# A decoder layer on one core: the FFN's down projection as seven block products, with operand sums made on GpSimd

## What is computed

```python
    x = x + mixed @ w_out[l]
    h2 = rmsnorm(x, norm_ffn_g[l])
    gate = causal_dwconv(h2 @ w_gate[l], ffn_conv_w[l]) + ffn_conv_b[l]
    x = x + (jax.nn.silu(gate) * (h2 @ w_up[l])) @ w_down[l]
return rmsnorm(x, norm_final_g)
```

## Time and profile before

| | us |
|---|---|
| median of three runs | 1390.34 (1389.62 to 1392.69) |
| the profiled execution | 1392.53 |
| its span, first to last instruction | 1390.7 |
| PE busy | 1318.5 (95%) |
| DVE busy | 863.5 (62%) |
| ACT busy | 576.2 (41%) |
| POOL busy | 332.6 (24%) |

### The profile page before, as it was taken

The page is one execution under the profiler, slowest core; times in us unless marked ns, Lnnn a source line. Parts: engine busy times, 40 slices in busy tenths (PEclk is TensorE's granted clock), DMA queues, the critical chain, the costliest instruction groups (busy, mean ns, idle before and its releaser), DMA issues.

```text
span 1390.7 us, 17095 instructions
## 1 busy us (share of the span) xinstructions
PE 1318.5 (95%) x6366; PEld 1076.2 (77%) x6366; DVE 863.5 (62%) x1195; ACT 576.2 (41%) x1028; POOL 332.6 (24%) x248
## 2 busy tenths in 40 slices
PE   7999999988888899889997999999999999999996
PEld 6788888876667687768886788888888878888885
DVE  6433352179887888654458888877777873345442
ACT  6211121078777787532353333333333332234330
POOL 0100100033131321100065455545445410001010
PEclk9999999999999999999999999999999999999998
DMA  5111112000000000143112222122222248435631
GB/s 220 53 45 45 61 46 91 0 20 1 1 1 1 1 2 1 49 169 131 63 40 80 91 74 75 64 91 91 74 78 92 76 157 298 157 118 167 202 97 61
DMA packets 37965, 110.75 MB, mean 80 GB/s; under 512 B 4016, under 2 KB 4528, under 8 KB 37680
## 3 DMA queue, kind: packets, MB, share of 16 engines
...
...
## 4 chain that ended last, share of the span: by engine, by line
PE 74%; DVE 13%; issue 6%; ACT 5%; POOL 1%; DMA 1%; DVEq 0%; SPq 0%; ACTq 0%; POOLq 0%
PE PS L496 9%; PE PS L497 8%; PE PS L500 8%; PE PS L2037 6%; PE PS L2039 6%; PE PS L2038 6%; PE PS L2049 6%; PE PS L2051 6%; PE PS L2050 6%; PE PS L1902 3%; DVE wl L1560 3%; ACT F L1053 2%; PE PS L1919 2%; DVE nmax L1439 2%; PE PS L1854 2%
## 5 line engine op out<-in xcount | busy, mean ns | idle before, releaser
L496 PE MATMUL PS<-R,wh 128*128 128x512 f32 x560 | 222.7, 398 | 13.7 <-DVE wl L488 13.7
L497 PE MATMUL PS<-R,wh 128*128 128x512 f32 x560 | 219.7, 392 | 0.0
L2037 PE MATMUL PS<-R,wh 128*128 128x512 f32 x480 | 189.3, 394 | 13.6 <-DVE wl L1560 8.4
L2038 PE MATMUL PS<-R,wh 128*128 128x512 f32 x480 | 188.1, 392 | 0.0
L2039 PE MATMUL PS<-R,wl 128*128 128x512 f32 x480 | 187.9, 392 | 0.0
L500 PE MATMUL PS<-R,wl 128*128 128x512 f32 x560 | 173.8, 392 | 0.0
L2049 PE MATMUL PS<-R,wh 128*128 128x512 f32 x352 | 137.5, 390 | 0.0
L2051 PE MATMUL PS<-R,wl 128*128 128x512 f32 x352 | 137.0, 389 | 0.0
L2050 PE MATMUL PS<-R,wh 128*128 128x512 f32 x352 | 137.0, 389 | 0.0
L496 PEld LDWEIGHTS PS<-R,wh 128*128 128x128 f32 x560 | 106.3, 190 | 37.6 <-DVE wl L488 14.6
L497 PEld LDWEIGHTS PS<-R,wh 128*128 128x128 f32 x560 | 106.3, 190 | 22.5 <-issue 0.7
...
## 6 DMA issues: line engine op xcount, KB each, us to landing
...
```

The lines of the kernel that those rows point to most:

```text
L496: nc.tensor.matmul(out, w_h, hi(kt)[:, cols], start=first, stop=False)
L497: nc.tensor.matmul(out, w_h, lo(kt)[:, cols], start=False, stop=False)
L2037: nc.tensor.matmul(out, w_h, operand(name, k, 0), start=fresh and k == 0, stop=False, skip_group_check=not fresh)
L2038: nc.tensor.matmul(out, w_h, operand(name, k, 1), start=False, stop=False, skip_group_check=not fresh)
```

## The change

The down projection is also done as 2 x 2 blocks in seven block products. The blocks are halves: the 22 tiles f pair up to eleven (even and odd tile of a pair are the two block rows of the inner dimension), the outputs split into d = 0 to 3 and 4 to 7, and the tokens into LEFT and RIGHT. Each of the seven products runs over the eleven pairs, so there are 77 steps, each of a 128 x 512 weight piece and a 128 x 512 activation piece, with four output banks and twelve matmuls. Products 0, 2, 4 and 6 add up in banks 0 to 3 without a clear, and 1, 3 and 5 use banks 4 to 7. DVE adds a bank group into the residual's quarters in the first steps of the next product, 28 additions of 128 x 512 before the last four; before it was 16 in all.

The weight sums S1 to S4 are made by POOL for the eleven pairs, at the very start and in the convolution stage behind L782: load two weight units (1 MB) by a DMA of its own queue into `R2`, four 128 x 512 operations, store the sums (1 MB) to DRAM. ACT waits for all the stores before it first writes `R2`. The activation sums T1 to T4 of a gated pair are made by POOL behind the S sums of m odd (`act_sums`): four 128 x 512 operations out of `SA`, then two DMA stores of 512 KB. ACT's silu of the next pair waits for them. SP stores three quarters of each pair (256 KB each) in place of two tiles, and SP's fetch of the residual now also waits for the last activation sums.

The splits run three steps ahead in place of two, in a ring of six half slots for the weights.

```diff
+        DOWN = (("A11", "B11"), ("S1", "T1"), ("S2", "T2"), ("S4", "B22"), ("S3", "T3"), ("A12", "B21"), ("A22", "T4"))
+        STEPS_DOWN = NP * PAIRS
+        TAIL_K = 4
+        HALF_D = KT // 2
+        D1, D3 = F1[:, 4, LEFT], F1[:, 4, RIGHT]
+        D2, D4 = PBm[:, 1024:1024 + BANK], PBm[:, 1024 + BANK:2048]
...
+        act_dram = nc.dram_tensor("gated", (NP, PAIRS, P, BANK), F32).ap()
+        s_dram = nc.dram_tensor("weight_sums", (PAIRS, P, 4 * BANK), F32).ap()
...
+            if v < SLOTS:
+                eng.wait_ge(p_done, NP * MATRICES + v - SLOTS + 1)
             else:
-                eng.wait_ge(dw_done, u - 4 + 1)
+                eng.wait_ge(dw_done, v - SLOTS + 1)
...
+            if v == 0:
+                return [2, 3]
+            if v == STEPS_DOWN - 5:
+                return [v + 3, v + 4]
+            return [n for n in [v + 3] if n < STEPS_DOWN - 1]
...
+                done = a_last if p == PAIRS - 1 else a_out
                 sp.wait_ge(a_ready, count)
-                sp.dma_start(a_dram[2 * p + e], SA[e]).then_inc(a_last if p == PAIRS - 1 else a_out, 16)
+                if e:
+                    sp.dma_start(act_dram[3][p], SA[1][:, LEFT]).then_inc(done, 16)
+                    sp.dma_start(act_dram[5][p], SA[1][:, RIGHT]).then_inc(done, 16)
+                else:
+                    sp.dma_start(act_dram[0][p], SA[0][:, RIGHT]).then_inc(done, 16)
...
             def load_down(v):
-                if v < 2:
+                q, k = divmod(v, PAIRS)
+                name = DOWN[q][0]
+                if v < 4:
                     sp.wait_ge(p_lo, NP * (MATRICES - 1))
-                elif v < 4:
-                    sp.wait_ge(p_lo, NP * MATRICES)
                 else:
                     sp.wait_ge(dw_lo, v - 3)
-                n = DOWN0 + v % FT if v < 2 * FT else LAST0 + v - 2 * FT
-                sp.dma_start(down_raw(v)[:, down_columns(v)], w_units[n][:, down_columns(v)]).then_inc(down_in[v % 4], 16)
+                if name[0] == "S":
+                    src = s_dram[k][:, (int(name[1]) - 1) * BANK:int(name[1]) * BANK]
+                else:
+                    src = w_units[DOWN0 + 2 * k + (name[2] == "2")][:, RIGHT if name[1] == "2" else LEFT]
+                sp.dma_start(down_raw(v), src).then_inc(down_in[v % 4], 16)
 
             def load_a(n):
+                q, k = divmod(n, PAIRS)
                 if n < 4:
                     sp.wait_ge(p_lo, NP * MATRICES)
                 else:
                     sp.wait_ge(da_lo, n - 3)
                 if n == 0:
-                    sp.wait_ge(a_out, 32 * (PAIRS - 1))
-                if n == FT - 2:
-                    sp.wait_ge(a_last, 32)
-                sp.dma_start(a_raw(n), a_dram[n % FT][:, half_of(n // FT)]).then_inc(a_in[n % 4], 16)
-
-            for v in range(3):
+                    sp.wait_ge(a_out, 48 * (PAIRS - 1))
+                if n == PAIRS - 1:
+                    sp.wait_ge(a_last, 48)
+                if n == PAIRS:
+                    sp.wait_ge(dt_out, 32 * (PAIRS - 1))
+                if n == 2 * PAIRS - 1:
+                    sp.wait_ge(dt_last, 32)
+                sp.dma_start(a_raw(n), act_dram[q][k]).then_inc(a_in[n % 4], 16)
...
+            for v in range(4):
                 load_down(v)
+            for v in range(4):
                 load_a(v)
...
                 if 6 <= v < 6 + KT:
                     if v == 6:
                         sp.wait_ge(p_done, NP * MATRICES)
-                        sp.wait_ge(a_last, 32)
+                        sp.wait_ge(a_last, 48)
+                        sp.wait_ge(dt_made, 4 * PAIRS)
                     sp.dma_start(x2(v - 6), x1_dram[v - 6]).then_inc(x1_back, 16)
...
+            def load_weights(p):
+                at = 4 * (p % 2)
+                pool.dma_start(W2[:, at:at + 2, :], w_units[DOWN0 + 2 * p:DOWN0 + 2 * p + 2].rearrange("u p n -> p u n"))\
+                    .then_inc(ws_in[p % 2], 16)
+
+            def weight_sums(p):
+
+                at = 4 * (p % 2)
+                a11, a21, a12, a22 = (W2[:, at + n, cols] for n in (0, 1) for cols in (LEFT, RIGHT))
+                s1, s2, s3, s4 = (W2[:, at + n, cols] for n in (2, 3) for cols in (LEFT, RIGHT))
+                pool.wait_ge(ws_in[p % 2], 16 * (p // 2 + 1))
+                if p > 1:
+                    pool.wait_ge(ws_out[p % 2], 16 * (p // 2))
+                nc.gpsimd.tensor_tensor(s1, a21, a22, ALU.add).then_inc(ws_made, 1)
+                nc.gpsimd.tensor_tensor(s3, a11, a21, ALU.subtract).then_inc(ws_made, 1)
+                pool.wait_ge(ws_made, 4 * p + 1)
+                nc.gpsimd.tensor_tensor(s2, s1, a11, ALU.subtract).then_inc(ws_made, 1)
+                pool.wait_ge(ws_made, 4 * p + 3)
+                nc.gpsimd.tensor_tensor(s4, a12, s2, ALU.subtract).then_inc(ws_made, 1)
+                pool.wait_ge(ws_made, 4 * p + 4)
+                pool.dma_start(s_dram[p], W2[:, at + 2:at + 4, :].rearrange("p u n -> p (u n)")).then_inc(ws_out[p % 2], 16)
+                if p + 2 < PAIRS:
+                    load_weights(p + 2)
+
+            load_weights(0)
+            load_weights(1)
+            weight_sums(0)
             pool.wait_ge(r_ready, 2)
             for i in range(CONV_T):
                 pool.wait_ge(conv_ready, i + 1)
                 nc.gpsimd.tensor_tensor(F1[:, CT_S, :], F1[:, CT_S, :], F1[:, R_S, :], ALU.mult).then_inc(tapr_ready, 1)
+                for p in range(1 + 3 * i - (i > 0), min(PAIRS, 3 + 3 * i)):
+                    weight_sums(p)
...
+            def act_sums(p):
+
+                pool.wait_ge(a_ready, folded(p, 4) if p else 2)
+                if p:
+                    pool.wait_ge(dt_out, 32 * p)
+                nc.gpsimd.tensor_tensor(D1, SA[0][:, LEFT], SA[0][:, RIGHT], ALU.subtract).then_inc(dt_made, 1)
+                nc.gpsimd.tensor_tensor(D3, SA[1][:, LEFT], SA[0][:, LEFT], ALU.subtract).then_inc(dt_made, 1)
+                pool.wait_ge(dt_made, 4 * p + 1)
+                nc.gpsimd.tensor_tensor(D2, SA[1][:, LEFT], D1, ALU.subtract).then_inc(dt_made, 1)
+                pool.wait_ge(dt_made, 4 * p + 3)
+                nc.gpsimd.tensor_tensor(D4, SA[1][:, RIGHT], D2, ALU.subtract).then_inc(dt_made, 1)
+                pool.wait_ge(dt_made, 4 * p + 4)
+                done = dt_last if p == PAIRS - 1 else dt_out
+                pool.dma_start(act_dram[1:5:3, p].rearrange("a p n -> p a n"),
+                               F1[:, 4, :].rearrange("p (a n) -> p a n", a=2)).then_inc(done, 16)
+                pool.dma_start(act_dram[2:7:4, p].rearrange("a p n -> p a n"),
+                               PBm[:, 1024:2048].rearrange("p (a n) -> p a n", a=2)).then_inc(done, 16)
...
             for m in range(0, MATRICES, 2):
                 for j in range(1, 5):
                     sum_of(m + 1, j)
+                act_sums(m // 2)
                 if m + 2 < MATRICES:
                     for j in range(1, 5):
                         sum_of(m + 2, j)
                 spread_silu(m + 3, 1)
                 spread_silu(m + 4, 0)
+            act_sums(PAIRS - 1)
+            pool.wait_ge(dt_last, 32)
...
+            act.wait_ge(ws_out[0], 16 * ((PAIRS + 1) // 2))
+            act.wait_ge(ws_out[1], 16 * (PAIRS // 2))
             for k in range(CONV_T):
                 act.wait_ge(yn_ready, k + 1)
                 nc.scalar.activation(R2[:, k, :], F1[:, Y0 + k, :], ACT.Copy).then_inc(mc_hi, 1)
...
                 if p:
-                    act.wait_ge(a_out, 32 * p)
+                    act.wait_ge(a_out, 48 * p)
+                    act.wait_ge(dt_made, 4 * p)
                 nc.scalar.activation(SA[e], T1[e], ACT.Silu).then_inc(silu_ready, 1)
...
+                if q and k == 0:
+                    dve.wait_ge(dw_done, q * PAIRS)
+                if q == 1 and k < 4:
+                    add_down(k, k, RIGHT)
+                if q == 2 and k < 8:
+                    add_down(4 + k % 4, k, LEFT)
+                if q == 3 and k < 4:
+                    add_down(k, k, LEFT, before=ADDS_OF_P1 + k + 1)
+                if q == 4 and k < 4:
+                    add_down(4 + k, k, LEFT, before=ADDS_OF_P5 + k + 1)
+                if q == 5 and k < 4:
+                    add_down(k, 4 + k, LEFT, before=ADDS_OF_P1 + 4 + k + 1)
+                if q == 6 and k < 4:
+                    add_down(4 + k, k, RIGHT, before=k + 1)
+                if v == NORM_AT:
...
+            def down_tile(v, d):
+
+                q, k = divmod(v, PAIRS)
+                w_h, w_l = (down_weight(w, v)[:, d * P:(d + 1) * P] for w in (wh, wl))
+                out, fresh = PS[:, 4 * (q % 2) + d, :], q == 0 or q % 2 == 1
+                nc.tensor.matmul(out, w_h, a_part(v, 0), start=fresh and k == 0, stop=False, skip_group_check=not fresh)
+                nc.tensor.matmul(out, w_h, a_part(v, 1), start=False, stop=False, skip_group_check=not fresh)
```

(20 more changed lines are left out.)

194 lines of the change are left out of this document (62 added, 132 removed).

## The result

The changed kernel takes 1367.40 us (median of 4 runs, 1366.64 to 1367.99), the kernel before 1391.51 (4 runs, 1389.62 to 1392.91): a ratio of 0.983 with a 95% interval from 0.982 to 0.984. The span of the profiled execution went from 1390.7 to 1366.2 us, 24.5 less.

What follows compares the result with a forecast made beforehand. The number of TensorE matmuls bounds the kernel, in gate and up a little DVE. Terms -29.9 + 14.3 - 0.5 + 0.7 + 1.0 = -14.4 us took the median from 1390.34 to 1376.0, range 1363 to 1389.

Steps and rivals of the forecast that it cites:

- Matmuls, -29.9: Down projection: 132 fewer matmuls at 0.2267 us each, all on TensorE's path, -29.9 us.
- L2127 to L2129: Sign in the page after: these down lines would show 924 matmuls at the same 0.2267 us.
- Nine pairs, +9.9: Gate and up: later S1 to S3 meet DVE's work, TensorE waits 1.1 us more per pair, +9.9 us (1.8 to 17).
- First pair, +4.4: Gate and up's first pair, DVE without idle time: four more contended POOL operations at 1.1, +4.4 us (1 to 5).
- Hand-over, -0.5 and +0.7: Entering down: shorter first weight split, -0.5 us (0 to -1); step 3's activation split late, +0.7 (0 to 3).
- Loads of down, +1.0: Early down: loads queued behind the residual's fetch reach step 14 about when TensorE wants it, +1.0 us (0 to 4).
- Weight sums, 0: Start and convolution: POOL's idle time takes the weight sums, done before ACT writes `R2`, +0 us (0 to 3).
- (a): Rival: activation sums fit into DVE's gaps (issues of 0.55 us or good order), 3 us instead of 14.3, 1364; chance 0.22.
- (b): Rival: more lost than counted, holds of 1.9 us a pair or loads late at step 14, 1383 to 1389; chance 0.18.
- (c): Rival: POOL issues slowly, 3.1 us each, delaying S1 and the weight sums; slower than before, 1398; chance 0.09.
- the forecast's 15 to 20: Sign: TensorE's waits for C22 would rise from 5.1 us to 15 to 20; near 8 would mean (a).
- (d): Rival: DVE becomes the bound of down, two splits of 1.50 us per step, +40 us, 1415; 0.06 with others.

Runs made afterwards that it cites:

- run with two memsets: Changed kernel with two write-only 256-column memsets between the activation sums' transfers and S1 in eight of ten pairs: 1373.37 us, ratio 0.987 to the kernel before.
- run with 512 rows: Changed kernel with each of POOL's eleven 1 MB weight-sum stores as 512 rows of 2 KB instead of 128 of 8 KB: 1369.14 us, single run.
- run of their own: Kernel before plus the weight sums alone, loaded, summed and stored by POOL but read by nobody, 1056 down matmuls kept: 1391.32 us, ratio 1.001.
- four memsets more: Changed kernel with four write-only 256-column memsets between the activation sums' transfers and S1 in eight pairs: 1375.42 us, ratio 0.989 to the kernel before.

## Why the prediction was right, and where not

**Matmuls, -29.9.** Right: 132 fewer at the same distance. 923 distances of 0.2267 are 209.2 us, and from 1138.68 to 1350.96 it is 212.3: 1.8 us are the final norm's matmuls in between, as in the kernel before, and 1.2 what is named below. The "L2127 to L2129" of the prediction are L2126 to L2128.

**Nine pairs, +9.9: measured +1.5** (0.17 in each of the seven periods that repeat, taken for nine). This is the term that was mis-sized, and nearly the whole miss. Two steps of its working failed. The first is the issue time. The prediction took 1.07 us for 256 rows, from a slope through 0.55 (20 rows) and 0.79 (128 rows). Those two rows are different transfers, and their difference was not one of rows (the second took 0.72 in the changed kernel). POOL and DVE of the changed kernel, answering to the earlier trace rows:

```profile
958.96 0.75 POOL L960 DMA_DIRECT2D gated<-F  x1 [0.30 <-POOL PBm L957]
959.71 0.73 POOL L962 DMA_DIRECT2D gated<-PBm  x1
960.46 1.30 POOL L937 TENSOR_TENSOR F<-raw 128x512 f32<-128x512 f32 x1
```

```profile
956.22 1.30 DVE L1624 TENSOR_TENSOR wl<-F,wh 128x512 fp32r<-128x512 f32 x1
...
958.03 1.18 DVE L1624 TENSOR_TENSOR wl<-F,wh 128x512 fp32r<-128x512 f32 x1
959.14 0.68 DVE L1702 TENSOR_TENSOR F<-F,PBm 128x512 f32<-128x512 f32 x1
...
969.38 0.68 DVE L1670 TENSOR_TENSOR raw<-PS,raw 128x512 f32<-128x512 f32 x1
```

The alternation came as worked out: D2 and D4 hold a split each, the readouts from PSUM run free. But the issues took 0.75 and 0.73, so S1 came 18.77 us after the restart and not 16.53 + 2.85 = 19.38. The second step is what follows S1. The run with two memsets puts S1 at 19.39, where the prediction had it, and its period is 39.36: 0.76 us lost a pair, not 1.1. So of the 0.94 us a pair between forecast and measurement (1.1 against 0.16), the issue time accounts for 0.60 and the working of DVE's path behind S1 for 0.34. The prediction's own working gave 0.2 for an issue of 0.55 us and 1.1 for 1.07; on the line between them 0.74 gives 0.5, three times the measured 0.16.

**First pair, +4.4.** The size was right, in part by luck: the waits went from 1.83 to 0.83 + 5.02 = 5.85, +4.0. The prediction made it of holds alone, four of 1.1. The runs make it of two things. With the issues alone in the kernel (no activation sums) the waits are 3.13, with memsets of the sums' length 3.60, so 1.8 of the 4.0 come without a hold by these four operations, and the hold adds 2.25, half of the 4.4. What the 1.3 us of the run without sums come from stays open; the issues' place ahead of S1 is hardly it, since with them behind S3 the first pair still waits 5.48. A little was added that the prediction had not counted: behind a wait TensorE runs at the lower clock. The stretches 775 to 780 us of the changed kernel and of the version whose first sums stand where DVE is idle too (the third column from the right is the granted clock):

```profile
775.00:780.00 5.00, 4.22 (x10) 3.39 (x11) 4.96 (x6) 1.90 (x3) 3.69 (x2) 0.50 0.40 134
```

```profile
775.00:780.00 5.00, 5.00 (x24) 4.14 (x23) 4.96 (x3) 1.96 (x4) 5.00 (x2) 1.00 0.61 210
```

It is 0.50 (1.2 GHz) behind the wait of 5.02 us, and 1.00 (2.4 GHz) where none stood just before. The stage's sum leaves 5.40 - 4.0 - 1.5 + 0.5 (next item) = 0.4 us for it. This part is what scatters: behind the wait of 5.02 us thirteen matmuls start 0.43 us apart (775.77 to 781.46), behind the same wait of 5.06 us in the run with 512 rows only seven (777.66 to 780.78), which is 1.2 us.

**Hand-over, -0.5 and +0.7.** Right: the last pair's wait fell from 1.24 to 0.71. Step 3 of down came late at 1147.25, 0.64 us (its activation split, L1714) behind the matmul before it instead of 0.23, some 0.5 with the gap after it.

**Loads of down, +1.0: measured about +0.6, elsewhere.** The prediction looked at step 14, by a count of bytes. The late ones are steps 7 and 8: their first matmuls start 0.40 and 0.49 us behind the one before (1158.42 and 1161.50) instead of 0.23. ACT's timeline has the reason for step 7, the activation's high part that waited for its load:

```profile
1156.92 0.63 ACT L1281 ACTIVATE R<-F 128x512 fp32r<-128x512 f32 x1 [2.07 <-DMA F<-gated]
```

Between 1135 and 1180 us the activations' loads took a median 7.8 us to land, 4.0 over the whole program. Together with the item above: 132 x 0.2267 = 29.9, less 28.68, is 1.2 us, which is these three places to 0.1. They scatter with the loads: over the ten kernels that have this down projection the third piece is 27.8 to 29.7 us under the old one's.

**Weight sums, 0.** Right (the run of their own). The rows that the prediction named: the groups stand one behind the other in POOL's idle time, 7.7 and 6.7 us from store to store (85.79, 93.44, 100.18) where 7.3 to 9 were foreseen, and the last store was issued at 158.15 us against a foreseen 164. The prediction let a sum and a DVE operation take turns; the split of 5.49 us shown above stood behind three of POOL's sums in a row (87.11 to 90.9), and no run shows why.

**Sum.** -29.9 + 4.0 + 0.4 + 1.5 - 0.5 + 1.2 = -23.3, and -1.3 from ahead of the stage, where it scatters: -24.6, against the measured -24.5. The range held because it was 26 us wide; the largest waiting term came out at a sixth of its size.

**The rivals.** (a) was nearest, in time (1364) and in TensorE's waits (9.8 us, against its 8 and the forecast's 15 to 20), and mostly for the reason it gave: issues far shorter than 1.07 us, if 0.74 and not 0.55. Part of its gain was that DVE's path behind S1 was too long in the working, which it did not say. (b) did not happen: even with four memsets more, S1 1.35 us later than in the changed kernel, a pair loses 1.24 us and not 1.9. (c) did not happen: beside DVE's tensor_tensor an issue took 0.75 us and not 3.1, and DVE's folds beside the issues (959.14) took 0.68. (The Trainium skill's inference that a tensor_tensor does not starve such a DMA, named in the prediction, agrees with these rows; its 3100 ns beside a tensor_copy no run here shows.) (d) did not happen: two splits of 0.77 and 0.76 us per step of 2.72. The chances hold a slip: (b) is 0.18 with half of it under 1387.5, yet 0.15 of it is counted as faster; with 0.09 the chance of faster is 0.76.
